# Attention of tiles 1 to 3 moved behind the first gathers of a two-layer encoder, heads in pairs, output weights loaded twice

## The reference, cut to what matters

```python
def stick_breaking_attention(q, k, v):           # 8 heads of 64
        z = jnp.einsum('bhqd,bhkd->bhqk', q_blk, kf) * scale
        causal = key_pos[None, :] < q_pos[:, None]
        log_keep = jnp.where(causal, jax.nn.log_sigmoid(-z), 0.0)
        later = lax.cumsum(log_keep, axis=3, reverse=True) - log_keep
        w = jnp.where(causal, jnp.exp(jax.nn.log_sigmoid(z) + later), 0.0)
        return jnp.einsum('bhqk,bhkd->bhqd', w, vf)
# even_layer: concatenate([att, gate_b * conv(gate_c * u)]) @ w_out
# peer_ffn, for each token:
        s = jnp.einsum('thpc,phkc->thpk', q, keys)
        sv, si = lax.top_k(s, PEER_TOPK)
        ...
        u = expert_u[idx]
        act = jax.nn.gelu(jnp.einsum('tnd,td->tn', u, hb).astype(jnp.float32))
        return jnp.einsum('tn,tnd->td', (gate * act).astype(expert_v.dtype), expert_v[idx])
```

## Time and profile before

| | |
|---|---|
| median of 3 runs | 3049.98 us (3047.11 to 3051.6) |
| the profiled execution: span on the core | 3049.0 us |
| TensorE busy | 1904.7 us (62%) |
| VectorE busy | 2095.4 us (69%) |
| ScalarE, GpSimd busy | 725.1 us (24%), 995.4 us (33%) |
| DMA: moved, mean rate | 1140.14 MB, 374 GB/s |
| of that, gathers of POOL's queue | 1090.59 MB |
| chain that ended last: DMA, TensorE, VectorE | 57%, 18%, 12% |

### The profile page before, as it was taken

How to read it: one execution, slowest core, us unless ns; L and a number is a source line. 1 busy time by engine, 2 the same in 40 slices (tenths; PEclk the granted TensorE clock), 3 DMA queues, 4 the chain that set the end, 5 groups by cost and what they waited for, 6 DMA issues and landing times.

```text
span 3049.0 us, 41865 instructions
## 1 busy us (share of the span) xinstructions
PE 1904.7 (62%) x13374; PEld 779.3 (26%) x13374; DVE 2095.4 (69%) x6444; ACT 725.1 (24%) x2829; POOL 995.4 (33%) x1112
## 2 busy tenths in 40 slices
PE   9999885755665466456565565556655566444444
PEld 4765322221222122122222222222222222111111
DVE  2143678996788668576788677866887588755556
ACT  2035122122212222123122222232222322121212
POOL 0000133333443333233333333333333333333332
PEclk9999997777876678677777787777877777667666
DMA  5131499999999999999999999999999999999998
GB/s 194 57 131 56 173 333 415 420 421 414 418 408 412 413 417 412 420 409 421 413 411 412 417 412 415 409 411 420 410 409 413 421 412 406 419 417 418 417 419 332
DMA packets 165492, 1140.14 MB, mean 374 GB/s; under 512 B 18672, under 2 KB 19696, under 8 KB 29856
## 3 DMA queue, kind: packets, MB, share of 16 engines
q0 software_dynamic: 149760, 1090.59, 87.3%
q1 hardware_dynamic: 15520, 46.94, 4.1%
HBM read 1135.30 MB, written 2.10 MB: 373 GB/s over the span
## 4 chain that ended last, share of the span: by engine, by line
DMA 57%; PE 18%; DVE 12%; issue 10%; ACT 1%; POOL 0%; POOLq 0%; DVEq 0%; SPq 0%
DMA ring_early<-in_peer_vu,idx_u 20%; DMA ring_early<-in_peer_uv,idx_u 18%; DMA ring_late<-in_peer_uv,idx_u 11%; DMA ring_late<-in_peer_vu,idx_u 8%; PE psum L1570 3%; DVE ring_early L1694 3%; PE psum L732 3%; PE psum L1125 3%; PE psum L1103 2%; PE psum L635 2%; PE psum L668 1%; DVE ring_late L1694 1%; DVE work L1242 1%; PE psum L597 1%; DVE si L1240 1%
## 5 line engine op out<-in xcount | busy, mean ns | idle before, releaser
L1694 DVE SCALAR_TENSOR_TENSOR ring_early<-ring_early,psum 128x1024 f32<-128x1024 f32 x704 | 856.5, 1217 | 439.0 <-DMA ring_early<-in_peer_uv,idx_u 220.6
L1570 PE MATMUL psum<-ring_early,w_col 128*32 128x256 f32 x5504 | 533.7, 493 | 716.8 <-ACT w_col L1629 687.1
L1694 DVE SCALAR_TENSOR_TENSOR ring_late<-ring_late,psum 128x1024 f32<-128x1024 f32 x336 | 409.0, 1217 | 218.3 <-DMA ring_late<-in_peer_uv,idx_u 135.8
L1491 POOL DMA_INDIRECT ring_early<-in_peer_vu,idx_u x352 | 330.6, 939 | 617.3 <-DVE ring_early L1694 366.3
L1491 POOL DMA_INDIRECT ring_early<-in_peer_uv,idx_u x352 | 330.4, 939 | 578.2 <-DVE ring_early L1694 383.1
L1570 PE MATMUL psum<-ring_late,w_col 128*32 128x256 f32 x2688 | 270.4, 498 | 373.6 <-ACT w_col L1629 354.2
L1570 PEld LDWEIGHTS psum<-ring_early,w_col 128*32 128x32 f32 x5504 | 189.4, 131 | 1093.3 <-issue 769.4
L1629 ACT ACTIVATE w_col<-block_fold,weight 128x32 f32<-128x32 f32 x1024 | 269.0, 313 | 664.5 <-DVE weight L1671 661.1
L1625 ACT ACTIVATE ge<-ga 128x4 f32<-128x4 f32 (+1 forms) x265 | 54.3, 205 | 1327.4 <-DVE ga L1655 1327.4
L1125 PE MATMUL psum<-wq,hbT 128*128 128x512 f32 x512 | 313.8, 702 | 0.8 <-ACT hbT L1058 0.8
L1491 POOL DMA_INDIRECT ring_late<-in_peer_uv,idx_u x168 | 157.5, 938 | 296.4 <-DVE ring_late L1694 250.5
(11 more groups left out here) (268 smaller groups left out, 2148.2 us busy)
## 6 DMA issues: line engine op xcount, KB each, us to landing
wq<-in_peer_w_query SPq DMA_DIRECT2D x16, 1024.0 KB, 18.8
w_ring<-in_even_w_in SPq DMA_DIRECT2D x5, 2048.0 KB, 7.9
ring_early<-in_peer_vu,idx_u POOLq DMA_INDIRECT x352, 12.9
ring_early<-in_peer_uv,idx_u POOLq DMA_INDIRECT x352, 12.9
w_ring<-in_even_w_out SPq DMA_DIRECT2D x1, 4096.0 KB, 14.2
ring_late<-in_peer_vu,idx_u POOLq DMA_INDIRECT x168, 12.9
ring_late<-in_peer_uv,idx_u POOLq DMA_INDIRECT x168, 12.9
hT<-in_x_T SPq DMA_DIRECT2D x4, 528.0 KB, 6.6
```

Of the source, the lines that this page charges most:

```text
L1491: nc.gpsimd.indirect_dma_start(pair_cells(at), None, uv_rows if at.side else vu_rows, bass.IndirectOffsetOnAxis(idx_u[par][:, i:i + 1], 0) ...
L1570: nc.tensor.matmul(block_part(b, n), w_col[:, i % W_SLOTS, :], v_cell(at)[:, part_cols(n)], start=False, stop=last, skip_group_check=True) ...
L1694: nc.vector.scalar_tensor_tensor(out=cell, in0=cell, scalar=1.0, in1=rows, op0=ALU.mult, op1=ALU.mult, accum_out=dot[par][:, i:i + 1]).the ...
```

## The change

The loop over heads is gone. The attention is cut into 24 units, worked through in order. Units 1 to 4 are tile 0 with its meta tokens, two heads each; units 5 to 8 are tile 1, two heads each; units 9 to 24 are tiles 2 and 3, one head each. The meta tokens' keys of the tiles before (16 keys, "tails") are a small extra step for all heads.

- Tile 0's transposes, scores, log-weight sums and outputs stand between the twelve convolution blocks. Units 5 to 8 stand in the meta routing.
- Units 9 to 24 are hooks at rows 1, 3, 6, 8, 11 and so on to 38. At each of them TensorE does the sums and the output of unit n and the scores of unit n + 2, ScalarE the matching passes; VectorE's softplus stands six rows on.
- Tile 0's output product is made in three parts, two of them behind the select of the meta indices. Gathers of rows 1 to 3 wait until the part of the first output weights that lies under their group is used.
- The output weights are loaded a second time, behind the last unit; the products of tiles 2 and 3 move from rows 0 to 29 to rows 49 to 84.
- Six pieces of the query weights are issued behind the last convolution step; keys and gain are loaded early; the ring of input weights has three slots.
- The four early groups serve 100 rows and not 36, in the order 3, 2, 0, 1. Until run 10 a fill uses one half alone and so waits for the last dot of the run before it.
- The norm of the meta rows for layer 1 moves from rows 30 and 37 to 84 and 90; some fills of constants go.

```diff
-EARLY_TILE_ROWS = 20
+EARLY_TILE_ROWS = 84
 EARLY_ROWS = CHUNK + EARLY_TILE_ROWS
-ORDER = ([n % GROUPS_EARLY for n in range(EARLY_ROWS)] +
-         [(GROUPS_EARLY + n) % RING for n in range(2 * XT * TILE_ROWS - EARLY_TILE_ROWS)])
+EARLY_ORDER = (3, 2, 0, 1)
+LATE_ORDER = (4, 5) + EARLY_ORDER
+ORDER = ([EARLY_ORDER[n % GROUPS_EARLY] for n in range(EARLY_ROWS)] +
+         [LATE_ORDER[n % RING] for n in range(2 * XT * TILE_ROWS - EARLY_TILE_ROWS)])
 
 
...
+        UNITS = ([(0, (2 * p, 2 * p + 1)) for p in range(HEADS // 2)] + [(1, (2 * p, 2 * p + 1)) for p in range(HEADS // 2)] +
+                 [(t, (h,)) for t in (2, 3) for h in range(HEADS)])
+        FIRST_UNITS, SECOND_UNITS, ALL_UNITS = HEADS // 2, HEADS, len(UNITS)
...
+        def unit_later(pe, n):
+            pe.wait_ge(s_sp, n + 1)
...
+            t, heads = unit(n)
+            w = unit_width(n)
+            add(unit_z(n), neg_tri[:, :], unit_sp(n))
+            for ahead in range(1, t + 1):
+                part = w - P * ahead
+                z3 = unit_z(n).rearrange("p (i n) -> p i n", n=w)
+                sp3 = unit_sp(n).rearrange("p (i n) -> p i n", n=w)
+                add(z3[:, :, 0:part], neg_ones[:, :], sp3[:, :, w - part:w])
+            for i, h in enumerate(heads):
+                tail = sp_tail[tail_rows(t), META * h:META * h + META]
+                ends = [w] if t == 0 else [P * b + P for b in range(t + 1)]
+                for end in ends:
+                    add(unit_z(n, i)[:, end - META:end], neg_ones[tail_rows(t), :], tail)
+                cut = P if t == 0 else P - META
+                at = 0 if t == 0 else P * t
+                last = add(unit_z(n, i)[:, at:at + cut], ident_b[:, :], neg[:, P - cut:])
+            last.then_inc(s_S, 1)
...
+        def unit_attend(pe, n):
+            t, heads = unit(n)
+            pe.wait_ge(s_w, n + 1)
+            apart(pe)
+            for h in heads:
+                i = heads.index(h)
+                nq = unit_width(n) if t == 0 else P
+                dst = psum[head_rows(h), unit_bank(n), 0:nq]
+                for b in range(t + 1):
+                    nc.tensor.matmul(dst, v_all[:, b, head_cols(h)], unit_sp(n, i)[:, P * b:P * b + nq],
+                                     start=(b == 0), stop=True, skip_group_check=True)
+            for h in heads:
+                nq = unit_width(n) if t == 0 else P
+                dst = psum[head_rows(h), unit_bank(n), 0:nq]
+                last = nc.tensor.matmul(dst[:, nq - META:nq], v_tail[tail_rows(t), head_cols(h)], w_tail[tail_rows(t), META * h:META * h + META],
+                                        start=False, stop=True, skip_group_check=True)
+            last.then_inc(s_av, 1)
...
+        def unit_logs(act, n):
+            act.wait_ge(s_z, FIRST_UNITS + 1 if n == TAILS else n + 1)
+            nc.scalar.activation(dst, src, ACT.Abs).then_inc(s_log, 1)
+            act.wait_ge(s_log, 3 * n + 1)
+            nc.scalar.activation(dst, dst, ACT.Exp, scale=-1.0).then_inc(s_log, 1)
+            act.wait_ge(s_log, 3 * n + 2)
+            nc.scalar.activation(dst, dst, ACT.Ln, bias=1.0).then_inc(s_log, 1)
...
+        def unit_softplus(dve, n):
+            dve.wait_ge(s_log, 3 * n + 3)
+            z, t = (tail_z, sp_tail[:, :]) if n == TAILS else (unit_z(n), unit_sp(n))
+            nc.vector.scalar_tensor_tensor(out=t, in0=z, scalar=0.0, in1=t, op0=ALU.max, op1=ALU.add).then_inc(s_soft, 1)
+            dve.wait_ge(s_soft, n + 1)
...
+        def unit_out(act, n):
+            t, heads = unit(n)
+            act.wait_ge(s_av, n)
+            rows = slice(0, P) if len(heads) == 2 else head_rows(heads[0])
+            nq = META + P if t == 0 else P
+            nc.scalar.copy(catT[rows, heads[0] // 2, unit_queries(n)], psum[rows, unit_bank(n), 0:nq]).then_inc(s_att, 1)
...
+        def run_half(f):
+            return 0 if f < SINGLE else (f + 1) % 2
+        def fill_at(f):
+            return CHUNK + RUN * f - (7 if f < SINGLE else 9 if f == SINGLE else FILL_AHEAD)
...
             pe.wait_ge(s_hb, job + 1)
+            pe.wait_ge(s_dot, CHUNK + RUN * (f if f < SINGLE else f - 1))
...
+        def w_out_sync(sp_):
+            sp_.wait_ge(s_att, ALL_UNITS)
+            sp_.dma_start(w_out_again[:, :, :], even_w_out[0].rearrange("(k p) n -> p k n", p=P)).then_inc(s_wout, 16)
...
+        def unit_at(n):
+            return 1 + 5 * (n - LATE_UNITS[0]) // 2
+        def unit_hooks_tensor(pe):
+            def step(n):
+                unit_later(pe, n)
+                unit_attend(pe, n)
+                if n + 2 <= ALL_UNITS:
+                    unit_scores(pe, n + 2)
+            return ([(unit_at(n), lambda n=n: step(n)) for n in LATE_UNITS] +
+                    [(PRODUCTS_AT + n, lambda n=n: project_step(pe, n)) for n in range(PRODUCTS)])
+        def unit_hooks_scalar(act):
+            def step(n):
+                unit_weights(act, n)
+                unit_out(act, n)
+                if n + 2 <= ALL_UNITS:
+                    unit_logs(act, n + 2)
+            return ([(unit_at(n), lambda n=n: step(n)) for n in LATE_UNITS] +
+                    [(PRODUCTS_AT + PRODUCT_STEPS * (i - 5), lambda i=i: take_projected(act, i)) for i in range(6, 10)] +
+                    [(PRODUCTS_AT + PRODUCTS + 1, lambda: move_hb_scalar(act))])
+        def unit_hooks_vector(dve):
+            first = [(1 + i, lambda i=i: unit_softplus(dve, LATE_UNITS[i])) for i in range(2)]
+            return first + [(unit_at(n) + 6, lambda n=n: unit_softplus(dve, n + 2)) for n in LATE_UNITS if n + 2 <= ALL_UNITS]
...
+            meta_project_tensor(pe)
+            unit_later(pe, 5)
+            unit_later(pe, 6)
+            start_tensor(pe, 0, META, 0)
+            unit_attend(pe, 5)
+            unit_attend(pe, 6)
+            meta_queries_tensor(pe)
+            pair_scores(pe, 7, 8, 3)
+            meta_queriesT_tensor(pe)
+            meta_scores_tensor(pe)
             project_tensor(pe, 2)
-            start_tensor(pe, 0, META, 0)
-            meta_queries_tensor(pe)
-            meta_scores_tensor(pe)
             project_tensor(pe, 3)
+            unit_later(pe, 7)
+            unit_later(pe, 8)
             meta_rows_tensor(pe)
-            project_tensor(pe, 4)
-            start_tensor(pe, 1, P, 0)
+            unit_attend(pe, 7)
+            unit_attend(pe, 8)
+            project_both_tensor(pe, 0)
             pe.wait_ge(s_routed, 2)
             meta_select_tensor(pe, top_i, META_IDX, s_midx)
+            project_both_tensor(pe, 1)
+            project_both_tensor(pe, 2)
+            start_tensor(pe, 1, P, 0)
             pe.wait_ge(s_hbT, 4)
             def first_query(s):
-                query_tensor(pe, first_piece(1) + s, s, P, 0, KD, (LATE_BANK, QUERY_BANK)[s])
+                query_tensor(pe, first_piece(1) + s, s, P, 0, KD, (QUERY_BANK, LATE_BANK)[s])
                 if s == 0:
                     pe.wait_ge(s_gate, 1)
                     meta_select_tensor(pe, soft, META_GATE, s_gateT)
...
+            extras = {1: [lambda: pair_tensor(pe, 0)], 2: [lambda: pair_tensor(pe, 1)], 3: [lambda: pair_tensor(pe, 2)],
+                      4: [lambda: pair_tensor(pe, 3)], 5: [lambda: pair_scores(pe, TAILS, 4, 1)],
+                      6: [lambda n=n: unit_later(pe, n) for n in range(3)], 7: [lambda n=n: unit_attend(pe, n) for n in (1, 2)],
+                      8: [lambda n=n: unit_later(pe, n) for n in (3, 4)], 9: [lambda n=n: unit_attend(pe, n) for n in (3, 4)],
+                      11: [lambda: pair_scores(pe, 5, 6, 2)]}
...
-            rows = ([n // 2 for n in range(16)] + [8, 9] + [11, 12, 13, 14, 15] +
-                    [CHUNK + n for n in range(4)] + [CHUNK + 5 + n for n in range(PRODUCT_STEPS)])
-            assert len(rows) == 4 * PRODUCT_STEPS
-            products = [(row, lambda n=n: project_step(pe, n)) for n, row in enumerate(rows)]
```

More of the change, by code:

```diff
@@ L180, in program @@
         odd_g = sb("odd_g", [P, KD])
+        with ExitStack() as again:
+            w_out_again = sb("w_out_again", [P, KD, D], where=again)
         pool_s = sb("pool_s", [P, D])
@@ L260, in program @@
         s_small = sem("small_loaded")
-        s_win = [sem(f"w_in_loaded{i}") for i in range(2)]
+        s_win = [sem(f"w_in_loaded{i}") for i in range(3)]
         s_wout = sem("w_out_loaded")
@@ L1489, in gather_pool @@
                     pool.wait_ge(s_acc, PARTS * at.summed)
+                if at.uses == 0 and at.group < len(OUT_ROWS):
+                    pool.wait_ge(s_wout_used, 1 + (2, 0, 1).index(at.group))
                 apart(pool)
```

663 lines of the change are left out of this document (334 added, 329 removed).

## The result

The changed kernel takes 3158.64 us at the median (3157.51 to 3159.95, 4 runs), the kernel before 3050.79 beside it: a ratio of 1.0355, interval 1.034 to 1.037. The prediction said slower, 3082 us with a range of 3036 to 3110. The sign was right; the size, 108 us and not 32, lies outside the range.

What follows compares the result with a forecast made beforehand. DMA was taken to bound the kernel from 629 us on, so only earlier time could change. Minus 44 (first sum), plus 42, 32 and 4 gave plus 34 on 3049, about 3082 us; range 3036 to 3110.

Steps and rivals of the forecast that it cites:

- First gather and first sum: Start of the kernel: first gather 61 us sooner, near 273.5 us; first sum 44 us sooner, near 319.5.
- Rows 0 to 40: Expert rows holding sixteen attention units: 42 us longer, at 16.5 us per batch of four rows, 165 us against 122.
- Rows 40 to 100: Expert rows on four buffer groups instead of six, one place for fills: 32 us longer, 3.1 us a row.
- Second load: Loading the output weights again, 4.19 MB: 4 us longer, ends 0 and 10.
- Units that hide: Rival: in rows 0 to 40 units fit TensorE's waits during gathers, ten batches under about 135 us; 3033 us, chance 0.2.
- Four groups that are enough: Rival: short gather latency lets four groups keep DMA busy, rows 40 to 100 stay at 2.57; about 3051 us, chance 0.1.
- TensorE as the bound of rows 49 to 84: Rival: output products, queries, sums and a blocking fill make TensorE the limit there, 3.6 us a row; 3105 us, chance 0.12.

## Why the prediction was wrong

**First gather and first sum: right in kind.** The last convolution block ends at 206.7 us (206 forecast). The first gather is 9 us later than forecast, 282.5. TensorE's wait for the query weights is as forecast (6.3 us, 6.5 forecast), though they land some 3 us later (the chain shows their DMA until 229.6), so what runs ahead of that wait takes longer too. Behind it TensorE runs the meta routing slower, at a clock of 0.78 from 229 to 247 us, with the meta queries at 8.78 us where the chain of the kernel before has 7.20. The rest of the 9 us is not traced; in the other profiles of the changed kernel and its variants the first gather stands between 281.8 and 286.6. From the gather to the sum it is 43.1 and not 46. Net 37.8 and not 44.

**Rows 0 to 40: the step that failed.** The prediction priced a batch of four rows at "1.6 x 7.3 = 11.7, plus four sums (2.6), plus half a fill", near 16, and took 16.5. From row 8 to row 40 a batch takes 24.0 us in the changed kernel (337.0 to 529.0) and 13.0 without units (325.1 to 428.8). The picture behind the price was right: the serial chain of units and sums on TensorE and ScalarE takes the place of the gathers' loop, whose transfers are then hidden. What failed is the list of what stands in that chain. Its pieces from 337.0 to 529.0 us, per batch:

| piece | forecast, us | in the chain, us |
|---|---|---|
| units (TensorE, ScalarE, softplus) | 11.7 | 13.0 |
| four sums | 2.6 | 3.0 |
| fill | 1.6 | 1.1 |
| routing of the next tile on TensorE (L1203, L1216, L1292) | none | 3.1 |
| other steps of ScalarE (columns, indices) and VectorE | none | 2.3 |
| hand-offs ("issue") | none | 1.6 |

The last three lines, 7.0 us a batch, had no term, and no reason was given for leaving them out. Of all TensorE's work only units, sums and the fill were counted. Without units the routing's queries (L1203 here) run while the gathers are under way and have 4.9 us of the chain of rows 0 to 40; behind units in the same queue they have 21.0.

Another reading fits the same figures, that a unit's time is added to the gathers' loop (13.0, and 11.0 for the units, make 24.0). But the 11.0 is itself the difference of the two, and the sum of a unit's parts and a gather's latency is not what the trace shows: the DMA engines are busy while units run, VectorE waits 4.6 us for gathers, and the chain has none. That the savings of both engines add doesn't decide between the two readings, as the chain leads through both engines in either. The account rests on the chain and the waits of one profiled execution of each kernel; no run took the routing out of these rows or made the gathers faster. What part the order within the queues has is not shown either: spreading each unit over three rows brought 5 us, moving and pairing them 26.

**Rows 40 to 100: mis-sized.** Forecast 32 for four groups and one half, and 4 for the second load; measured 50.5. In the kernel before, four groups make these rows 23.5 us longer (2.96 a row) and the one half 13.9 more, 37.4 in all, or 3.19 a row where the prediction took 3.1. Without units the changed kernel has 41.1. The other 9.4 come with the last two units, which end at 548.8, behind the dot of row 40, and the second load, which the run without units has ahead of the rows; their shares are not shown. The prediction put all sixteen units into the rows before. (Another 10 of the 110 that the units cost stand ahead of the first sum.)

**Second load: 4 forecast,** 1.4 measured at the median; 4 is not excluded.

**The sum itself** is a little off. Its terms make 34, so 3083 and not 3082; 165 less 122 is 43 and not 42; and 80 less 6.5, 3.4 and 9.7 is 60.4. None of this matters beside the miss.

**The rivals.** Units that hide are out: ten batches take 203 us and not under 135, though the gathers do hide beside them. Four groups that are enough are out. The 5.6 us which that rival took for a gather alone belong to the first of four that were issued within 4 us (334.40 to 338.29), so a gather alone is shown nowhere. TensorE as the bound of rows 49 to 84 was not the mechanism: from 529 to 733 it is busy for 155 of 204.5 us, no more of it than in the four-group stretch before (55.7 of 64), and gathers hold 67.6 us of the chain there.

## What to carry to other kernels

A gap beside a transfer is seldom empty. Work that is moved into it may hide the transfer and still cost its whole length, when the loop's other work, which had run in that gap, now stands behind it in the same queues. So when the moved work ties up two engines in turn, price a batch as the sum of all that stands on those two queues (here units, sums, fill, routing, columns and hand-offs), and compare that sum with the transfer's loop. And count what the move takes away: here two buffer groups and a half of PSUM for 64 more rows cost the 39 us that the earlier start had won.

## What the runs showed of the hardware that was not expected

TensorE's granted clock changed the price of the log-weight sums more than their shapes did. In the block of units ahead of the rows, sums of a pair of tile 2 took 4.77 us at a granted clock of 1.00. Of tile 3 the same 34 instructions took 12.08 us in one pair, at a granted clock of 0.56 over the window, and 6.93 us in another, at 1.00, although TensorE had been idle for 2.5 us ahead of both. What decides between them isn't shown. Over rows 0 to 40 the granted clock was 0.92 in the kernel before, 0.76 in the changed kernel, 0.80 with paired units, 0.66 with little TensorE work in them and 0.70 without units, so in all of these TensorE runs part of the time at the lower of its two levels (1.2 GHz).
